# The modulation product in plain fp32 on four column groups of TensorE, its weights unsplit

## The reference, cut to what matters

```python
for l in range(2):
    mod  = silu(c)     @ w_mod[l] + b_mod[l]     # w_mod[l]: 1024 x 6144
    modc = silu(c_ctx) @ w_mod[l] + b_mod[l]
    sh1, sc1, gt1, sh2, sc2, gt2 = split(mod, 6)         # 1024 each; modc likewise
    h  = rms_norm(xl, g_pre_mix[l]) * (1 + sc1) + sh1
    y, yc = token_mixer(h, hc, ...)                      # conv, attention and pool branches
    xl = xl + gt1 * rms_norm(y, g_post_mix[l])
    h  = rms_norm(xl, g_pre_ffn[l]) * (1 + sc2) + sh2
    xl = xl + gt2 * rms_norm(swiglu(h, ...), g_post_ffn[l])
```

## Time and profile before

| | us |
|---|---|
| median of 3 runs | 2652.38 |
| lowest and highest run | 2650.01 and 2653.25 |
| profiled execution, first to last instruction (span) | 2649.7 |
| PE busy in it | 2375.7 (90%) |
| DVE, ACT, POOL busy | 1533.1, 998.0, 188.5 |
| mean granted TensorE clock | 0.927 |

### The profile page before, as it was taken

One profiled execution on the slowest core, in us unless ns is written; L12 is line 12 of the kernel. 1 busy time (PEld: TensorE's weight loads), 2 busy tenths in 40 slices (PEclk: granted clock), 3 DMA queues, 4 the chain that ended last, 5 costly groups with the idle time before them and its releaser, 6 DMA issues. The chain is left out here.

```text
span 2649.7 us, 33281 instructions
## 1 busy us (share of the span) xinstructions
PE 2375.7 (90%) x12945; PEld 1968.0 (74%) x12945; DVE 1533.1 (58%) x2379; ACT 998.0 (38%) x1613; POOL 188.5 (7%) x233
## 2 busy tenths in 40 slices
PE   5879978999979999996897898999789899898998
PEld 2666746777757777776775787997777898787997
DVE  4499376654454444236936666564675565654564
ACT  4322265342243333223226444333343343343333
POOL 1052100000010000003310000000100000000000
PEclk7899999999989999997998999999785999886999
DMA  7222202444324445233320465564530466341564
GB/s 222 64 72 64 77 8 74 133 120 135 112 80 156 148 157 159 88 95 108 104 80 21 140 181 165 167 183 135 151 99 17 143 183 197 114 128 32 165 182 138
DMA packets 440191, 317.71 MB, mean 120 GB/s; under 512 B 25770, under 2 KB 379732, under 8 KB 440036
## 3 DMA queue, kind: packets, MB, share of 16 engines
q1 hardware_dynamic: 438500, 310.79, 39.2%
q0 software_dynamic: 1504, 4.79, 0.6%
q10 hardware_dynamic: 32, 0.01, 0.0%
HBM read 314.50 MB, written 1.05 MB: 119 GB/s over the span
## 5 line engine op out<-in xcount | busy, mean ns | idle before, releaser
L276 DVE TENSOR_TENSOR split<-raw,split 128x1024 fp32r<-128x1024 f32 (+1 forms) x602 | 718.0, 1203 | 754.4 <-ACT split L273 752.9
L287 PE MATMUL PS<-HH,split 128*128 128x256 f32 (+1 forms) x2504 | 819.8, 327 | 63.2 <-DVE HL L281 38.4
L273 ACT ACTIVATE split<-raw 128x1024 fp32r<-128x1024 f32 (+1 forms) x602 | 611.5, 1031 | 594.5 <-PE PS L289 473.3
L288 PE MATMUL PS<-HL,split 128*128 128x256 f32 (+1 forms) x2504 | 810.0, 323 | 0.0
L289 PE MATMUL PS<-HH,split 128*128 128x256 f32 (+1 forms) x2504 | 809.5, 323 | 0.0
L287 PEld LDWEIGHTS PS<-HH,split 128*128 128x128 f32 x2504 | 481.0, 192 | 116.6 <-DVE HL L281 41.6
L289 PEld LDWEIGHTS PS<-HH,split 128*128 128x128 f32 x2504 | 481.4, 192 | 38.0
L288 PEld LDWEIGHTS PS<-HL,split 128*128 128x128 f32 x2504 | 480.1, 192 | 38.9
L287 PE MATMUL PS<-split,UH 128*128 128x512 f32 x440 | 172.3, 391 | 0.0
L288 PE MATMUL PS<-split,UH 128*128 128x512 f32 x440 | 171.2, 389 | 0.0
L289 PE MATMUL PS<-split,UL 128*128 128x512 f32 x440 | 171.2, 389 | 0.0
(11 more groups left out here) (238 smaller groups left out, 2848.2 us busy)
## 6 DMA issues: line engine op xcount, KB each, us to landing
raw<-in_w_in_dram SPq DMA_DIRECT2D x120, 512.0 KB, 4.0
raw<-in_w_mod_dram SPq DMA_DIRECT2D x96, 512.0 KB, 4.5
raw<-in_w_ffn_in_dram SPq DMA_DIRECT2D x88, 512.0 KB, 3.9
raw<-in_l_w_gate_up_dram SPq DMA_DIRECT2D x88, 512.0 KB, 3.9
raw<-in_w_ffn_out_dram SPq DMA_DIRECT2D x44, 512.0 KB, 3.5
raw<-in_l_w_down_dram SPq DMA_DIRECT2D x44, 512.0 KB, 4.2
raw<-in_l_w_in_dram SPq DMA_DIRECT2D x30, 512.0 KB, 4.6
raw<-in_w_attn_out_dram SPq DMA_DIRECT2D x16, 512.0 KB, 4.3
```

Source lines behind the costliest of these rows:

```text
L273: eng.activation(c["high"], c["raw"], ACT.Copy).then_inc(high_done, 1)
L276: eng.tensor_tensor(c["low"], c["raw"], c["high"].bitcast(F32), ALU.subtract).then_inc(low_done, 1)
L287: pe.matmul(out, a[0], b[0], start=first, stop=False)
L288: pe.matmul(out, a[0], b[1], start=False, stop=False)
```

## The change

The product keeps fp32 operands and gives up the split. `silu_c` becomes a plain fp32 stationary of 32 columns for each k (two used, the rest zero, set by a new memset on POOL). A step is now one row of 128 of `w_mod` for 1024 columns, again one chunk of 512 KB, loaded with `split=False`. It is four plain fp32 matmuls of 256 columns, number j writing PSUM partitions 32j to 32j + 31. Eight steps make a group of 1024 columns, and there are 12 groups. A group is copied as 128 x 256, turned by two transposes of 128 x 128, and DVE picks two columns of each 32 out of the result. Layer 1's last groups move from its branches into layer 0's FFN, which now has 7 groups, 56 steps, at its 44 points: one each, and two at every third point. `pick`, `silu_f` and their split and load go.

```diff
-    groups = [(l, s, n) for l in range(DEPTH) for s in range(6) for n in range(2)]
-    phases = {"start": groups[0:4], "L0_branches": groups[4:10], "L0_ffn": groups[10:21], "L1_branches": groups[21:24]}
+    groups = [(l, s) for l in range(DEPTH) for s in range(6)]
+    phases = {"start": groups[0:2], "L0_branches": groups[2:5], "L0_ffn": groups[5:12]}
...
+    def mod_steps(phase, point):
+
+        if phase not in phases:
+            return []
+        steps = [point]
+        if phase == "L0_ffn":
+            steps = [point + point // 3] + ([point + point // 3 + 1] if point % 3 == 2 else [])
+        return [q for q in steps if q < KT * len(phases[phase])]
...
-        i, ws = T.load(rows(A["w_mod"][l], k0, 2, sec * D + n * 512, 512), (2, 512))
...
-        for k in range(2):
-            for part in range(2):
-                ins = pe.matmul(bank(("mod",) + group)[0:4, :], silu_c[:, k0 + k, :], ws[part][:, k, :],
-                                start=(k0 + k + part == 0), stop=(k0 + k + part == KT))
+        for q in mod_steps(phase, point):
+            if q % KT == 1 and q > KT:
+                mod_turn(T, pe, phases[phase][q // KT - 1])
+            l, sec = group = phases[phase][q // KT]
+            k = q % KT
+            i, w = T.load(rows(A["w_mod"][l], k, 1, sec * D, D), (1, D), split=False)
+            if k == 0:
+                T.open(("mod",) + group)
+            for j in range(4):
+                ins = pe.matmul(bank(("mod",) + group)[QUAD * j:QUAD * (j + 1), 0:SEQ], silu_c[:, k, :],
+                                w[:, 0, SEQ * j:SEQ * (j + 1)], start=(k == 0), stop=(k == KT - 1))
...
-        for k in range(4):
-            ins = pe.matmul(ps[:, 2 * k:2 * k + 2], row[:, k * P:(k + 1) * P], pick[:, :], start=True, stop=True)
+        for h in range(2):
+            ins = pe.transpose(ps[:, h * P:(h + 1) * P], row[:, h * P:(h + 1) * P], ident[:, :])
...
-        read_out(act.activation(MR[:, g % 2, :], bank(("mod",) + group)[0:4, :], ACT.Copy), ("mod",) + group)
+            read_out(act.activation(MR[:, g % 2, :], bank(("mod",) + group)[:, 0:SEQ], ACT.Copy), ("mod",) + group)
...
+        pool.memset(silu_c[:], 0.0).then_inc(S("silu_zeroed"), 1)
...
-        split_value(dve, silu_c[:, :, 0:2], silu_c[:, :, 2:4], silu_f[:, :, :]).then_inc(S("silu_c"), 1)
-        dve.wait_ge(S("consts"), 16 * 2)
-        split_until(dve, GROUP)
+        dve.wait_ge(S("consts"), 16)
...
-        others[4 * GROUP] = load_x
+        others[2 * KT] = load_x
```

More of the change, by code:

```diff
@@ L65 @@
 SLOT = 1024
+QUAD = 32
 RAW = (3, 5)
@@ L113, in shape_constants @@
         "causal": causal.reshape(2, P, SEQ), "dilated": dil.reshape(2, P, 3, SEQ),
-        "freqs": freqs, "pick": sel,
+        "freqs": freqs,
     }
@@ L455, in build @@
     G = sb("G", [P, 2, D])
-    pick = sb("pick", [4, 2])
-    silu_f = sb("silu_f", [P, KT, 2])
-    silu_c = sb("silu_c", [P, KT, 4], F32R)
+    silu_c = sb("silu_c", [P, KT, QUAD])
     mod = sb("mod", [P, DEPTH, 6, KT, 2])
@@ new lines, in build @@
+    phases = {"start": groups[0:2], "L0_branches": groups[2:5], "L0_ffn": groups[5:12]}
[6 more added lines that the diff above has]
+        return [q for q in steps if q < KT * len(phases[phase])]
+    def mod_pe(T, pe, phase, point):
+        for q in mod_steps(phase, point):
[9 more added lines that the diff above has]
+                                w[:, 0, SEQ * j:SEQ * (j + 1)], start=(k == 0), stop=(k == KT - 1))
+            if k < KT - 1:
+                T.mark(ins)
+            else:
+                T.close(ins, ("mod",) + group)
+            T.used(i)
@@ L597, in mod_act @@
[L597 to L602, removed]
-        read_out(act.activation(MR[:, g % 2, :], bank(("mod",) + group)[0:4, :], ACT.Copy), ("mod",) + group)
+        for q in mod_steps(phase, point):
+            if q % KT != KT - 1:
+                continue
+            group = phases[phase][q // KT]
+            g = groups.index(group)
+            wait_result(act, ("mod",) + group)
+            if g >= 2:
+                wait_result(act, ("turn",) + groups[g - 2])
+            read_out(act.activation(MR[:, g % 2, :], bank(("mod",) + group)[:, 0:SEQ], ACT.Copy), ("mod",) + group)
@@ L605, in mod_dve @@
     def mod_dve(dve, phase, point):
-        q = mod_step(phase, point)
-        if q is not None and q % GROUP == 1 and q > GROUP:
-            mod_columns(dve, phases[phase][q // GROUP - 1])
+        for q in mod_steps(phase, point):
+            if q % KT == 1 and q > KT:
+                mod_columns(dve, phases[phase][q // KT - 1])
     def mod_columns(dve, group):
-        l, sec, n = group
+        l, sec = group
         key = ("turn",) + group
         wait_result(dve, key)
-        b = 32 + 48 * l + 8 * sec + 4 * n
@@ L616, in mod_columns @@
[L616 to L618 removed]
+        b = 32 + 48 * l + 8 * sec
+        out = mod[:, l, sec, :, :].rearrange("p (j h) m -> p j h m", j=4)
+        turned = bank(key)[:, 0:SEQ].rearrange("p (h j c) -> p j h c", h=2, j=4)[:, :, :, 0:2]
@@ L619, in mod_columns @@
+        read_out(dve.tensor_tensor(out, turned, cols_mod[:, b:b + KT].rearrange("p (j h o) -> p j h o", j=4, o=1).broadcast_to([P, 4, 2, 2]),
+                                   ALU.add), key)
+        if sec in (SHIFT_1, SHIFT_2):
             return
-        wait_read(dve, ("turn", l, sec, 0))
         wait_read(dve, key)
@@ L623, in mod_columns @@
             part = int(sec == SCALE_2)
-            for half_ in range(2):
-                wait_read(dve, ("turn", l, sec - 1, half_))
+            wait_read(dve, ("turn", l, sec - 1))
             g0 = ROW_FFN if part else ROW_PRE
@@ L779, in _ @@
         T.close(pe.transpose(bank(("c",))[:, 0:2 * KT], stage_c, ident[0:2 * KT, 0:2 * KT]), ("c",))
-        pe.wait_ge(S("silu_c"), 1)
-        for q in range(GROUP * len(phases["start"])):
+        wait_read(pe, ("c",))
+        for q in range(KT * len(phases["start"])):
             mod_pe(T, pe, "start", q)
@@ L893, in _ @@
             branch(L + "yb", 2, 1, A["w_attn_out"][l], 8, (OTH, OTL), lambda: pe.wait_ge(S(L + "ot_parts"), 2 * len(tiles)))
-            mod_turn(T, pe, phases[L + "branches"][-1])
+            if L + "branches" in phases:
+                mod_turn(T, pe, phases[L + "branches"][-1])
             pe.wait_ge(S(L + "merged"), KT)
@@ L911, in _ @@
         act.wait_ge(pe_done, milestones[("c",)])
-        read_out(act.activation(silu_f[:, :, :].rearrange("p k m -> p m k"), bank(("c",))[:, 0:2 * KT].rearrange("p (m k) -> p m k", m=2),
+        act.wait_ge(S("silu_zeroed"), 1)
+        read_out(act.activation(silu_c[:, :, 0:2].rearrange("p k m -> p m k"), bank(("c",))[:, 0:2 * KT].rearrange("p (m k) -> p m k", m=2),
                                 ACT.Silu), ("c",))
-        for q in range(GROUP * len(phases["start"])):
+        for q in range(KT * len(phases["start"])):
             mod_act(act, "start", q)
@@ L924, in _ @@
             L = "L%d_" % l
-            keep_splitting(act, ("turn", l, SCALE_1, 1))
+            keep_splitting(act, ("turn", l, SCALE_1))
             act.wait_ge(S(L + "gains"), 1)
@@ L1013, in _ @@
                     gates_act(act, l, 0)
-            wait_result(act, ("turn",) + phases[L + "branches"][-1])
+            if L + "branches" in phases:
+                wait_result(act, ("turn",) + phases[L + "branches"][-1])
             post_act(act, L, "y", tiles)
-            keep_splitting(act, ("turn", l, SCALE_2, 1))
+            keep_splitting(act, ("turn", l, SCALE_2))
             act.wait_ge(S(L + "gains"), 2)
@@ L1280, in _ @@
                     gates_dve(dve, l, 0)
-            mod_columns(dve, phases[L + "branches"][-1])
+            if L + "branches" in phases:
+                mod_columns(dve, phases[L + "branches"][-1])
             post_dve(dve, L, "y", tiles, 0)
```

31 lines of the change are left out of this document (2 added, 29 removed).

## The result

| | before | after |
|---|---|---|
| median, us | 2652.43 | 2663.42 |
| lowest and highest, us (4 runs each) | 2650.01 to 2653.25 | 2660.80 to 2666.95 |
| profiled span, us | 2649.7 | 2663.7 |

A forecast was written before the change was run, and what follows sets the result against it. PE was taken as the bound, busy 90% of the span, with loads bounding the start. Terms -8.4 + 21 - 20 - 4 = -11.4 us on the 2649.7 span gave 2638.3, so a 2641 us median; range 2620 to 2682.

The forecast's parts named there:

- Step, 0.8 us: New modulation step on PE: four column groups side by side plus switching cost 0.8 us, against 0.92 before.
- two signs that were to show me wrong: Layer 0's FFN: PE's waits of 1.5 to 1.7 us behind double steps missing, or a step over 1.0 us.
- single file: Rival: column groups of a step don't overlap, a step takes 2.05 us, sum +72, 2724 us; chance 0.14.
- half overlap: Rival: one group's second record delays the next group's first, step 1.4 us, sum +19, 2671 us; chance 0.12.
- Turn 0.3: Turn of a finished modulation group on PE: two transposes and a load take 0.3 us, against 1.07 before.
- Start -4: Start, bound by loads: 4 us less, as the slot's loop loses ACT's and DVE's splits and gains PE's step.
- Layer 0's branches -8.4: Layer 0's branches: 24 cheaper steps give -2.9 us, three turns for six give -5.5, together -8.4.
- no stall: Layer 0's branches: the next gate is ready 3.3 us after the last, covered by PE's work with 0.3 to spare.
- Layer 1's branches -20: Layer 1's branches: losing 12 steps and 3 turns saves 14.2 us on PE, and 6 of waits; together -20.
- Layer 0's FFN +21: Layer 0's FFN: PE's work 293.3 us plus 25.4 of waits, against 297.6 before, makes it 21 us slower.
- The other stages, 0: Stages besides the start, both layers' branches and layer 0's FFN: no term in the sum, 0 us.
- 25 us of waits: Layer 0's FFN: PE waits 7 x 1.5 and 7 x 1.7 us behind double steps, plus 3 for raw slots: 25.4.

The follow-up runs named there:

- e4: Kernel before the change, old split fp32r product kept, with only the move of groups into layer 0's FFN, two steps at every third point: 2665.59 us, ratio 1.0050.
- e5: Changed kernel with two column groups of 64, two products of 512 columns a step and four transposes a turn: 2671.10 us, ratio 1.0071.
- e6: Changed kernel with eight products, their result overwritten, issued on PE ahead of the wait behind each pair in layer 0's FFN: 2652.52 us, ratio 1.0000.
- e1: Changed kernel with ACT and DVE both splitting one chunk further ahead where two unsplit steps stand behind a split chunk: 2640.12 us, ratio 0.9953.
- e2: Changed kernel with only ACT, not DVE, splitting one chunk further ahead at pairs of unsplit steps: 2652.10 us, ratio 1.0001.

## Why the prediction was wrong

- **Step, 0.8 us: right.** From product to product 0.88 to 0.90 us in place of 0.23, and 0.11 more inside the next chunk (its first two records start 0.34 apart, not 0.23): 0.78. I had forecast 1.0 from product to product; the difference is where those 0.11 stand. Neither of the two signs that were to show me wrong came, then: a step is under 1.0, and the waits are there. The records of the four column groups start 7 ns apart (769.568, 769.575, 769.581, 769.588), those of the second pass at 769.808. So single file and half overlap were both out. The Trainium skill's rule in "TensorE: Matmul & The Clock Gate", Part 3, Packing small matmuls, that a weight load overlaps a running matmul only where the row groups differ, does not describe this: the four products share all rows, and the second group's load starts at 769.573, while the first group's matmul (769.568 to 769.971) runs. The gain of 2.38 that the same section gives for three column tiles fits better: here four gave 1.91 / 0.64 = 3.0.
- **Second step of a pair: not foreseen.** It adds 0.43 us, not 0.8, since the switch to small tiles is paid once. I counted two full steps as cover. The splits came when I said, 3.1 and 3.3 us behind the end of the chunk ahead.
- **Turn 0.3: near.** It is 0.31 from the turn's start to the step's, but 0.09 of that is the step's own way in, so it adds 0.22. **Start -4: low** (-8.8). The loads ran at 276 GB/s, not 241, for one of the two reasons above. **Layer 0's branches -8.4: -5.0.** PE's waits for splits there grew from 0.9 to 2.9 us; "no stall" was 2 us too good. Another 1.3 is the distance between starts in its products on `CS`, `MIX`, `OTH` and `OTL`, 0.228 to 0.230 us before and 0.232 to 0.233 after. **Layer 1's branches -20: right** (-23).
- **Layer 0's FFN +21: wrong, and the step of the prediction that failed.** Its mechanism, the look-ahead counted in chunks, was right, and the waits stood where it put them, behind 14 pairs. They were mis-sized: PE's own work is 246.4 + 28 x 0.78 + 14 x 1.21 + 7 x 0.22 = 286.7 (forecast 293.3), and the waits are 14 x 2.17 + 2.7 = 33.1 us (forecast 25.4). The sum of the two, 319.8, is only 1.1 above the forecast's, for the reason the prediction itself gave: a faster pair is only waited for. The three kinds of step of the changed kernel, e4 and e5 show it: 3.35, 3.36 and 3.36 us across a pair. The term that was left out, put at nothing without a reason, is the clock: 11 slow stretches of 1.55 us each, 17 us. The total, 336.8 - 297.6 = 39.2, is 1.3 us over the measured 37.9. e6 takes the clock's part away alone, and e1 takes it and 12 us of the waits: with the same product and the same move it is 2640, 12 us faster than before.
- **The other stages, 0: wrong by 13 us** in the profiled execution. 10.4 of them stand in the y and down products: some 7 in the longer distance between their starts, 3 in the clock. By these sums, without these 10 and the FFN's 17 the kernel would have come out some 13 us faster, near the forecast.

The forecast's direction thus hung on 25 us of waits that were seen, and on nothing being behind them. That a range up to 2682 held the time is luck: it was made so wide for the half overlap, which didn't come.

## What to carry over

Where helpers work ahead by a count of chunks, two short chunks in a row push the next long one out of their reach, and then the time between long chunks is fixed: a faster short step buys nothing, and the idle time can cost a second time through the clock. Price a new wait of PE with what the granted clock does behind it; if it can't be removed, even useless products in it pay. Put small extra work where the engine idles already for another's result (16 steps for 7 us here, 47 in the busiest stage), and before a step is made unsplit, ask how long it holds its slot when the chunks around it are short. Compare the stages that you didn't touch as well: here they held 13 us.

## What was not expected of the hardware

- A wait of TensorE of 2.0 to 2.8 us behind two small-tile steps was followed, 0 to 1.4 us after it resumed, by 3.4 us at the lower clock level in 11 of 14 cases, and one of 2.2 us in e2 in 4 of 7. Waits behind two steps of 1.1 to 1.3 us (e4, e5), of 0.9 to 1.8 (e1) and of 1.5 to 1.8 (e2) were followed by none, and neither were the same steps with the wait filled (e6). Length of the wait is not all: ahead of layer 0's y product 1.2 us, with 0.5 shortly before, were followed by one, at 677.9 us.
- Plain fp32 records of four column groups of 32 run fully side by side: eight in 0.64 us with the tail, against 1.91 in one group. Two groups of 64, 512 columns each, make a pair of steps 0.86 us longer.
- Where a slot's loop is only load and product, the start's loads ran at 276 GB/s, against 241 with the splits in it and with 2 KB runs in place of 4 KB; which of the two did it is open.
- Products whose code was untouched changed their pace: 528 matmuls of the down product start 0.234 us apart where it was 0.227, at the same granted clock. The cause is open.
